# Last stage of a decoder layer: the first expert's rows added to h ahead of the running tile's second gating half

## What is computed

```python
# y: rows of all experts, two per token (top 2 of a group), weights: 2 per token
h = h + hier_moe(rmsnorm(h, g_ffn), ...)                      # h2 = h + w0*y[first] + w1*y[second]
h = h + jax.nn.sigmoid(h @ w_pg) * rmsnorm(p @ w_ple, ple_g)  # h3
y_prompt = rmsnorm(h, final_norm_g)                           # out
```

## Time and profile before

| | |
|---|---|
| median of 3 runs | 2298.84 us |
| the profiled execution, its own time | 2294.15 us |
| span of the profiled execution | 2292.6 us |
| TensorE busy | 2188.5 us, 95% |
| VectorE busy | 1486.0 us, 65% |
| ScalarE busy | 979.7 us, 43% |
| GpSimd busy | 409.1 us, 18% |
| granted clock of TensorE, mean | 0.974 |
| last stage | from 2016.2 us (first copy of row numbers) to the end |

### The profile page before, as it was taken

One profiled execution on the slowest core, in us unless ns is written; L12 is line 12 of the kernel. 1 busy time (PEld: TensorE's weight loads), 2 busy tenths in 40 slices (PEclk: granted clock), 3 DMA queues, 4 the chain that ended last, 5 costly groups with the idle time before them and its releaser, 6 DMA issues. The chain is left out here.

```text
span 2292.6 us, 33598 instructions
## 1 busy us (share of the span) xinstructions
PE 2188.5 (95%) x10675; PEld 1797.1 (78%) x10676; DVE 1486.0 (65%) x2863; ACT 979.7 (43%) x1575; POOL 409.1 (18%) x564
## 2 busy tenths in 40 slices
PE   6999999999899999996889999999999999989998
PEld 5888888888688888884678888888888888867775
DVE  4787777777656666555454557696665667846564
ACT  4433334334332222223444455575554555733332
POOL 1021100110234333232110000000000000023332
PEclk9999999999899999998899999999999999999999
DMA  6101101111624433324795759597775779844431
GB/s 227 58 38 65 64 32 64 64 64 69 223 102 120 141 123 133 102 88 151 255 371 197 279 182 372 212 394 289 292 290 189 283 286 363 326 174 170 156 132 53
DMA packets 161710, 412.40 MB, mean 180 GB/s; under 512 B 18931, under 2 KB 22443, under 8 KB 161390
## 3 DMA queue, kind: packets, MB, share of 16 engines
q1 hardware_dynamic: 139894, 342.41, 41.7%
q0 software_dynamic: 14560, 43.11, 5.5%
q10 hardware_dynamic: 7200, 26.22, 2.8%
HBM read 333.26 MB, written 86.92 MB: 183 GB/s over the span
## 5 line engine op out<-in xcount | busy, mean ns | idle before, releaser
L235 PE MATMUL bank<-w_hi,mix_x 128*128 128x512 f32 x816 | 338.0, 414 | 9.6 <-DMA mix_x<-xT_dram 4.0
L237 PE MATMUL bank<-w_hi,mix_x 128*128 128x512 f32 x816 | 328.6, 403 | 0.0
L2246 DVE TENSOR_TENSOR w_lo<-raw,w_hi 128x2048 fp32r<-128x2048 f32 x132 | 296.7, 2286 | 48.0 <-ACT w_hi L2181 48.0
L236 PE MATMUL bank<-w_lo,mix_x 128*128 128x512 f32 x816 | 327.6, 401 | 0.0
L2146 PE MATMUL bank<-w_hi,x_hi 128*128 128x512 f32 x784 | 305.9, 390 | 2.1 <-DVE x_lo L2238 2.1
L2148 PE MATMUL bank<-w_hi,x_lo 128*128 128x512 f32 x784 | 305.8, 390 | 0.0
L2147 PE MATMUL bank<-w_lo,x_hi 128*128 128x512 f32 x784 | 305.7, 390 | 0.0
L2181 ACT ACTIVATE w_hi<-raw 128x2048 fp32r<-128x2048 f32 x132 | 247.6, 1930 | 22.5 <-DMA raw<-in_w 22.4
L235 PEld LDWEIGHTS bank<-w_hi,mix_x 128*128 128x128 f32 x816 | 159.8, 196 | 43.2 <-issue 5.0
L237 PEld LDWEIGHTS bank<-w_hi,mix_x 128*128 128x128 f32 x816 | 158.6, 194 | 35.4
L236 PEld LDWEIGHTS bank<-w_lo,mix_x 128*128 128x128 f32 x816 | 160.0, 196 | 31.2
(11 more groups left out here) (318 smaller groups left out, 4108.1 us busy)
## 6 DMA issues: line engine op xcount, KB each, us to landing
raw<-in_w SPq DMA_DIRECT2D x128, 1024.0 KB, 8.8
shared<-in_w SPq DMA_DIRECT2D x64, 1024.0 KB
y_dram<-y_sb ACTq DMA_DIRECT2D x50, 512.0 KB
xT_dram<-mix_x SPq DMA_DIRECT2D x34, 512.0 KB, 3.5
mix_x<-xT_dram SPq DMA_DIRECT2D x34, 512.0 KB, 4.4
shared<-in_w_in SPq DMA_DIRECT2D x24, 512.0 KB, 6.6
small<-in_x_prompt SPq DMA_DIRECT2D x16, 512.0 KB
xr_sb<-in_x_prompt SPq DMA_DIRECT2D x16, 512.0 KB
```

The source lines that it names most:

```text
L235: pe.matmul(bank[:, :], x_hi[:, k, :], wh[:, k, :], start=(k == 0), stop=False)
L236: pe.matmul(bank[:, :], x_hi[:, k, :], wl[:, k, :], start=False, stop=False)
L237: ins = pe.matmul(bank[:, :], x_lo[:, k, :], wh[:, k, :], start=False, stop=(k == KD - 1))
L2246: dve.tensor_tensor(w_lo[slot(j, m)][:, cols], raw[raw_place(e, m)][:, cols], w_hi[slot(j, m)][:, cols].bitcast(F32), ALU.subtract).then_i ...
```

## The change

`combine` is split in two. Its first half adds the first expert's weighted rows to h in place, in h_in[b], and still stands behind both DMA waits (the load of h and the two gathers of tile t+2). In `tile` it is moved up: it stands behind `hT_half(t + 1)` and ahead of the wait for the second gate half. The new `combine_rest` adds the second expert's rows and writes h2[b]; it stands behind h3, where `combine` stood. For tiles 0 and 1 both halves still follow each other ahead of the loop. No other engine's program is touched.

```diff
                     def combine(t, turn, b, r):
+
                         dve.wait_ge(hp_sem[b], 16 * turn + 16)
                         dve.wait_ge(yg_sem[b], 32 * turn + 32)
-                        w = lambda n: wtok[0:r, n, bass.ds(t, 1)]
-                        STT(h2[b][0:r, :], y1[b][0:r, :], w(0), h_in[b][0:r, :], ALU.mult, ALU.add).then_inc(h2_part, 1)
+                        STT(h_in[b][0:r, :], y1[b][0:r, :], wtok[0:r, 0, bass.ds(t, 1)], h_in[b][0:r, :], ALU.mult, ALU.add).then_inc(h2_part, 1)
+
+                    def combine_rest(t, b, r):
                         dve.wait_ge(h2_part, t + 1)
-                        STT(h2[b][0:r, :], y2[b][0:r, :], w(1), h2[b][0:r, :], ALU.mult, ALU.add).then_inc(h2_ready, 1)
+                        STT(h2[b][0:r, :], y2[b][0:r, :], wtok[0:r, 1, bass.ds(t, 1)], h_in[b][0:r, :], ALU.mult, ALU.add).then_inc(h2_ready, 1)
...
                             if n == 0 and r1:
                                 hT_half(t + 1, 1 - b, r1)
+                            if n == 0 and r2:
+                                combine(t + 2, turn + 1, b, r2)
...
                         if r2:
                             dve.wait_ge(h3_ready, t + 1)
-                            combine(t + 2, turn + 1, b, r2)
+                            combine_rest(t + 2, b, r2)
...
                     combine(0, 0, 0, P)
+                    combine_rest(0, 0, P)
                     hT_half(0, 0, P)
                     combine(1, 0, 1, P)
+                    combine_rest(1, 1, P)
```

## The result

The changed kernel takes 2328.38 us (median of four runs, 2327.08 to 2330.33), the kernel before 2299.03 us (four runs, 2296.9 to 2299.59). The ratio is 1.013, with a 95% interval of 1.0113 to 1.0148: slower by 1.3%. Its profiled execution took 2328.34 us with a span of 2326.8 us.

The account below looks back on a forecast made before the run. TensorE alone was taken as the bound from tile 6 (15.47 us a tile), a circle through h2 before. Adding 19.0 and 12.4 us, together 31, to 2294.15 gave 2325, plus 4.7 us 2330; range 2316 to 2344.

Parts of the forecast that it names:

- The new circle: h3, squares, h3_rstd, gathers, landing, combine, gating, scaling and next h3 wait on each other: 17.2 us a tile.
- From h3 to the second gather's issue: End of h3 to GpSimd's second gather issue: 5.62 us early, 5.96 to 6.20 in the loop, less GpSimd's saving.
- the sum: Added stage time: 19.0 us in tiles 1 to 6 and 12.4 us in tiles 7 to 13, together 31 us.
- L2411 falls to 0.57 us: GpSimd's instruction, 1.32 or 1.63 us before, shortens as VectorE finishes sooner: 4.5 us saved early, 7.2 us later.
- The landings: Second gathers, issue to landing: 45.6 us for tiles 1 to 6, 52.2 us for tiles 7 to 13.
- the rival that hung on it: Both gathers in 4.6 us after the second issue, so hidden and the kernel faster: 2290 us; chance 4%.
- From the combine to the end of h3: On VectorE, combine's start through gating and scaling to the end of h3: 4.58 us a tile.
- the two parts: Tiles 1 to 6 take 103.1 us (before 84.1), tiles 7 to 13 take 120.7 us (before 108.3).
- TensorE's slack: TensorE's own turn is 15.1 us, so it waits about 2.1 us a loop tile, about 5 in tiles 1 to 5.
- the dearer case: GpSimd gains nothing, or TensorE's clock stays low two episodes a tile: +43 or +39 us, 2342 or 2338; 14%.
- The load of h: SyncE's load goes out in the same microseconds as the gathers; the gather was taken as the later of the two.
- The median: Profiled execution of 2294.15 us becomes 2325; keeping the median's 4.7 us distance above it gives 2330 us.

Follow-up runs that it names:

- the additional addition: The changed kernel with one more VectorE addition of two SBUF rows (result unused) right behind the combine's second half; 2337.97 us, ratio 1.0169.

## Why the prediction was right, point by point

- *The new circle.* Right, and shown: moving the fetches alone takes the loss away and turns it into a gain, moving the wait behind the gating half, still on the circle, leaves 20.0 of the stage's 31.0 us, and writing in place has no part in it. The chain of waits after names the same steps.
- *From h3 to the second gather's issue.* 4.87 us worked out for the early tiles and 4.97 to 5.14 for the loop; 4.85 to 4.90 and 4.97 to 4.98 measured. The loop came out shorter because L2409, too, which took 0.33 us in every second loop tile beside the combine, fell to 0.20; this was not in the sum. The prediction's 5.62 us before did not hold in tile 3, where the combine came late: 6.39 us, with 0.78 us for L2409 and 1.51 for L2411. With the combine gone from there tile 3 went like the others, so the sum did not suffer.
- *L2411 falls to 0.57 us.* Right in every tile. That a VectorE instruction beside it was the reason is shown by the additional addition. The Trainium skill ("GPSIMD Engine Reference", Key points) names contention with VectorE instructions that read two SBUF inputs; the trace agrees. Beside L2531, which has one of its two inputs in PSUM (2162.81 to 2164.10), L2407 took 0.22 us at 2163.32, no more than the 0.25 us at 2034.98 with VectorE idle.
- *The landings.* Taken from before one by one, 97.8 us for thirteen; measured 99.6 (6.8, 7.7, 7.9, 9.5, 7.5, 7.7, then 7.3, 7.4, 7.7, 7.6, 7.8, 7.3, 7.5). The fit in the Trainium skill ("DMA: Bandwidth & Descriptors", Anatomy of one DMA) makes an estimate of 3.2 us for 512 KB; no gather of 128 rows took under 5.0 us in the traces of before and after, none of the thirteen under 6.8, and the rival that hung on it did not happen. The prediction called the gather of 5.2 us alone on the queues, which it was not: another gather had been issued 1.26 us ahead of it, and a load of h of 512 KB moved in the same microseconds. What a gather takes alone, no run shows.
- *From the combine to the end of h3.* 4.58 us was 0.12 too long: the gating starts 1.20 us behind the combine, not 1.32, since it has no wait left to sit out. The landings were 1.8 us more than taken, so that the two nearly cancel: 103.7 and 119.8 us for the two parts against 103.1 and 120.7.
- *TensorE's slack.* 2.1 us a loop tile was too much: the waits for `em1` were up to 1.7 us, 12.6 us in nine. About 5 us in each of tiles 1 to 5 was too much as well: the waits for h2 were 4.2, 2.8, 5.3 and 4.8 us in tiles 1 to 4, and tile 5 has one for `em1`. In the loop the clock stayed at 1.00, so the dearer case did not arise. In tiles 1, 3 and 4 it was 0.50 for 3.5 us or more behind the wait, and this hid in the next wait, as worked out: in every tile the gating still followed the combine by 1.20 us.
- *The load of h.* The prediction took the gather as the later transfer, and that held for the changed kernel. That the load came almost as late was not seen: its landing has no row before, since nothing waited for it. It would have mattered to anyone who fetched only the gathers sooner: that kernel is 18 us slower than the one with both sooner.
- *The median.* 2330 forecast, 2328.38 measured; the stage grew by 31.0 as worked out, the medians by 29.4. The profiled execution was put at 2325 us and took 2328.34, by the 3.2 us in front of the stage, and the 4.7 us that were kept between it and the median were not there this time. That the forecast of the median is so close owes something to these two cancelling.

## What to carry to other kernels

Before a wait is moved ahead in an engine's stream, ask not only whether its inputs are there by then, but whether what stands behind it releases the issue of those very inputs. If so the latency of the fetch, here about 7.5 us, becomes part of every turn, however much slack the engine showed. The cure is to issue the fetch a turn sooner, as soon as the buffer is free, for every transfer in the wait: the move that cost 29 us then gave a kernel 11.6 us faster than the one it started from. In the stage that is 8.9 us, 2.6 from the sooner fetches by themselves and 6.3 from the move.

## What the runs showed of the hardware

- A one-column GpSimd instruction of 0.57 us took 1.33 us, and one of 0.19 us took 1.13 us, when it started 0.32 and 0.14 us behind a VectorE addition of two SBUF rows of 1.22 us: in both cases it ended behind the addition, by 0.43 and 0.05 us. In these rows the one that was hit started behind the addition: L2409, which in that loop tile started 0.07 us ahead of the addition, kept its 0.20 us.
- A longer wait of TensorE did not always lower its clock. After 4.23 us the granted clock was 0.50 for the next 3.5 us, after 2.77 us in the next tile it was 1.00, and yet in the kernel before it was 0.51 for 3.5 us after a wait of only 1.98 us:

```profile
2086.83:2090.30 3.47, 3.47 (x20) 3.01 (x21) 2.50 (x4) 2.70 (x7) 2.18 (x4) 1.00 0.10 13
2069.76:2073.30 3.54, 3.54 (x13) 3.15 (x14) 2.56 (x4) 2.80 (x7) 2.23 (x5) 0.50 0.12 50
```

- The thirteen second gathers, all of 512 KB, landed after 6.8 to 9.5 us in one execution, the longest beside loads of embedding rows, of h and of p and a store.
